# Next round's gather ahead of the up products, and split transfers for a turn's last couple, in a one-core hybrid decoder layer

## The reference, cut to what matters

```python
def per_sequence(args):
    hs, cs = args                                   # hs (256, 1024), cs (256, 32): weight of each expert, 0 if not chosen
    a = jnp.einsum('sd,edf->sef', hs, w_gate)       # w_gate, w_up (32, 1024, 256)
    u = jnp.einsum('sd,edf->sef', hs, w_up)
    act = jax.nn.silu(a) * u * cs[..., None].astype(hs.dtype)
    return jnp.einsum('sef,efd->sd', act, w_down)   # w_down (32, 256, 1024)
```

## Time and profile before

| | |
|---|---|
| device time, median of 3 runs | 353.47 us (353.11 to 355.06) |
| the profiled execution: device time / span | 353.66 us / 351.8 us |
| TensorE busy / VectorE / ScalarE / GpSimd | 90% / 48% / 35% / 13% of the span |
| DMA | 121.07 MB, mean 344 GB/s over the span |
| first gate matmul of the expert loop | 150.54 us |
| first matmul of the last pass / end of its downs | 329.84 us / about 341.85 us |

### The profile page before, as it was taken

One profiled execution on the slowest core, in us unless ns is written; L12 is line 12 of the kernel. 1 busy time (PEld: TensorE's weight loads), 2 busy tenths in 40 slices (PEclk: granted clock), 3 DMA queues, 4 the chain that ended last, 5 costly groups with the idle time before them and its releaser, 6 DMA issues.

```text
span 351.8 us, 11516 instructions
## 1 busy us (share of the span) xinstructions
PE 316.0 (90%) x4758; PEld 246.2 (70%) x4759; DVE 167.3 (48%) x461; ACT 121.4 (35%) x308; POOL 46.8 (13%) x82
## 2 busy tenths in 40 slices
PE   8999999999999999978799899999999849686582
PEld 6999899799774446666577677777777537556250
DVE  4868275554264513754345355555555422251333
ACT  2725264454254227333233133333333211220213
POOL 3300002632504037800000000000000000000001
PEclk9999999999999999999999999999999976898999
DMA  7999995081749998699999999999999999999953
GB/s 271 328 360 386 387 391 215 32 328 38 321 149 388 300 400 334 238 286 392 420 410 396 415 420 408 417 420 414 427 411 422 408 415 422 414 422 416 416 208 119
DMA packets 34709, 121.07 MB, mean 344 GB/s; under 512 B 5640, under 2 KB 10144, under 8 KB 27520
## 3 DMA queue, kind: packets, MB, share of 16 engines
q1 hardware_dynamic: 34352, 120.63, 88.1%
q10 hardware_dynamic: 336, 0.14, 0.1%
HBM read 119.72 MB, written 1.05 MB: 343 GB/s over the span
## 4 chain that ended last, share of the span: by engine, by line
PE 72%; DMA 11%; SPq 10%; issue 3%; ACT 2%; DVE 1%; POOLq 0%; POOL 0%; ACTq 0%; DVEq 0%
PE bank L815 13%; PE bank L555 13%; PE bank L622 7%; DMA spare<-in_w_up_dram 6%; PE bank L847 6%; PE bank L770 6%; DMA ring<-in_w_up_dram 5%; SPq L397 5%; PE bank L549 5%; PE bank L777 3%; SPq L409 2%; SPq L391 2%; PE bank L569 2%; PE bank L531 2%; PE bank L584 1%
## 5 line engine op out<-in xcount | busy, mean ns | idle before, releaser
L815 PE MATMUL bank<-ring,hT 128*32 128x128 f32 x1664 | 56.5, 290 | 15.1 <-DMA ring<-in_w_up_dram 7.5
L815 PEld LDWEIGHTS bank<-ring,hT 128*32 128x32 f32 x1664 | 49.6, 117 | 24.3 <-issue 24.1
L1557 DVE SCALAR_TENSOR_TENSOR yb<-bank,pp,yb 64x512 fp32r<-64x512 f32 x34 | 25.5, 750 | 47.8 <-ACT yb L1085 47.2
L1271 DVE TENSOR_TENSOR unit_lo<-ring,unit_hi 128x2048 fp32r<-128x2048 f32 (+1 forms) x12 | 26.5, 2209 | 24.0 <-ACT unit_hi L917 24.0
L770 PEld LDWEIGHTS bank<-pp,qk 128*128 128x128 bf16 x912 | 29.6, 101 | 7.4 <-issue 5.6
L1085 ACT ACTIVATE yb<-bank,pp 64x512 fp32r<-64x512 f32 x34 | 23.2, 683 | 32.3 <-PE bank L847 31.9
L770 PE MATMUL bank<-pp,qk 128*128 128x64 bf16 x912 | 31.9, 197 | 2.6 <-issue 2.6
L622 PE MATMUL bank<-ring,qk 128*128 128x512 f32 (+1 forms) x72 | 29.9, 551 | 0.0
L1233 POOL TENSOR_SCALAR stats<-qk 128x1 f32<-128x1 f32 x2 | 0.6, 310 | 197.2 <-ACT work L1105 197.2
L1540 DVE SCALAR_TENSOR_TENSOR pp<-bank,stats,pp 128x128 f32<-128x128 f32 x18 | 6.3, 351 | 43.0 <-ACT pp L1074 43.0
L815 PE MATMUL bank<-work,hT 128*32 128x128 f32 x320 | 19.7, 273 | 6.7 <-DMA spare<-in_w_up_dram 4.2
(11 more groups left out here) (217 smaller groups left out, 529.5 us busy)
## 6 DMA issues: line engine op xcount, KB each, us to landing
ring<-in_w_up_dram SPq DMA_DIRECT2D x24, 1024.0 KB, 17.2
ring<-in_w_down_dram SPq DMA_DIRECT2D x24, 1024.0 KB, 17.6
ring<-in_w_gate_dram SPq DMA_DIRECT2D x16, 1024.0 KB, 16.2
ring<-in_w_in_dram SPq DMA_DIRECT2D x4, 2048.0 KB, 17.3
ring<-in_w_gate_dram SPq DMA_DIRECT2D x16, 512.0 KB, 14.4
ring<-in_w_out_dram SPq DMA_DIRECT2D x4, 1024.0 KB, 13.7
spare<-in_w_gate_dram SPq DMA_DIRECT2D x4, 1024.0 KB, 18.7
spare<-in_w_up_dram SPq DMA_DIRECT2D x4, 1024.0 KB, 19.6
```

What stands on the lines that cost most here:

```text
L815: last = mm(p_gu[b:b + CAP, w * P:(w + 1) * P], hg[:, k, CAP * e:CAP * (e + 1)], w_gu[at[e]][:, w, k, h, :], start=(k == 0), stop=(k == KD ...
L1271: V.tensor_tensor(unit_lo[b][:, k, :], unit_src(u)[:, k, :], unit_hi[b][:, k, :].bitcast(fp32), ALU.subtract).then_inc(w_lo_ready, 1)
L1557: V.scalar_tensor_tensor(out=yb[half][rest, :], in0=p_y[rows, :], scalar=wcol[rows, :], in1=yb[half][rows, :].bitcast(fp32), op0=ALU.mult, ...
```

## The change

In TensorE's pass the gather of the next pass, with the read of `base` and the wait for `sel_ready` ahead of it, moves from behind the ups to between the small matmuls (L825) and the ups. Behind the ups come the selections, then `add_result`, and only then the wait for `act_ready` and the transpose. VectorE's and ScalarE's programs are the same. For the last couple of a turn the ups and the downs of each expert are loaded in two transfers of 512 KB instead of one of 1 MB: first the first halves of both experts, then the second ones, each half with a semaphore of its own, and TensorE waits for the second halves in the middle of the ups and of the downs.

```diff
+        dn2_in = {p: sem(f"dn2_in{p}") for p in places(TURN - 1)}
+        up2_in = {p: sem(f"up2_in{p}") for p in places(TURN - 1)}
...
+            def load_up_part(e, p, part):
+                c = slice(part * KD // 2 * FE, (part + 1) * KD // 2 * FE)
+                src = I["w_up"][0, bass.ds(e, 1)].rearrange("o (p k) f -> p (o k f)", p=P)
+                up = gu_at[p].rearrange("p (w c) -> p w c", w=2)[:, 1]
+                sp.dma_start(up[:, c], src[:, c]).then_inc((up_in, up2_in)[part][p], 16)
+
+            def load_dn_part(e, p, f):
+                src = I["w_down"][0, bass.ds(e, 1), f * P:(f + 1) * P].rearrange("o p n -> p (o n)")
+                sp.dma_start(w_dn[p][:, f], src).then_inc((dn_in, dn2_in)[f][p], 16)
...
                     sp.wait_ge(used, passed)
+                    if w == 1 and loads[0][1] in places(TURN - 1):
+                        for part in range(2):
+                            for e, p in loads:
+                                load_up_part(e, p, part)
+                        continue
...
                 sp.wait_ge(down_done, passed)
-                for e, p in loads:
-                    load_dn(e, p)
+                if loads[0][1] in places(TURN - 1):
+                    for f in range(2):
+                        for e, p in loads:
+                            load_dn_part(e, p, f)
+                else:
+                    for e, p in loads:
+                        load_dn(e, p)
...
                         if w == 0 and k == KD // 2:
                             pe.wait_ge(hg_ready, i + 1)
+                        if w == 1 and k == KD // 2 and at == places(TURN - 1):
+                            for e in range(2):
+                                pe.wait_ge(up2_in[at[e]], fillings * 16)
...
                         picked.then_inc(rr_done, 1)
-                pe.wait_ge(base_ready, 1)
-                pe.reg_load(edge, base[0:1, bass.ds(q + 1, 1)])
-                pe.wait_ge(sel_ready, i + 2)
-                gather(p_hg).then_inc(gathered, 1)
+
+                        pe.wait_ge(base_ready, 1)
+                        pe.reg_load(edge, base[0:1, bass.ds(q + 1, 1)])
+                        pe.wait_ge(sel_ready, i + 2)
+                        gather(p_hg).then_inc(gathered, 1)
                 pe.wait_ge(rrow_ready, i + 1)
                 pe.wait_ge(selw_ready, i + 1)
...
+                add_result(i)
                 pe.wait_ge(act_ready, i + 1)
                 nc.tensor.transpose(p_tr[:, 2 * P:3 * P], act_sb, ident).then_inc(actt_done, 1)
-                add_result(i)
                 pe.wait_ge(actT_ready, i + 1)
-                for e in range(2):
-                    pe.wait_ge(dn_in[at[e]], fillings * 16)
                 for f in range(2):
+                    if f == 0 or at == places(TURN - 1):
+                        for e in range(2):
+                            pe.wait_ge((dn_in if f == 0 else dn2_in)[at[e]], fillings * 16)
```

More of the change, by code:

```diff
@@ L405, in load_gu, with load_up @@
                     load_half(e, p, 0)
-                load_half(e, p, 1)
-            def load_dn(e, p):
-                sp.dma_start(w_dn[p], I["w_down"][0, bass.ds(e, 1)].rearrange("o (h p) n -> p (o h) n", p=P)).then_inc(dn_in[p], 16)
+                load_up(e, p)
+            def load_up(e, p):
+                if p in places(TURN - 1):
+                    load_up_part(e, p, 0)
+                    load_up_part(e, p, 1)
+                else:
+                    load_half(e, p, 1)
+            def load_up_part(e, p, part):
[6 more added lines that the diff above has]
+                sp.dma_start(w_dn[p][:, f], src).then_inc((dn_in, dn2_in)[f][p], 16)
+            def load_dn(e, p):
+                if p in places(TURN - 1):
+                    load_dn_part(e, p, 0)
+                    load_dn_part(e, p, 1)
+                else:
+                    sp.dma_start(w_dn[p], I["w_down"][0, bass.ds(e, 1)].rearrange("o (h p) n -> p (o h) n", p=P)).then_inc(dn_in[p], 16)
             def load(e):
@@ L445, in _ @@
             sp.wait_ge(lo_ready, LAST)
-            load_half(RINGED, RINGED, 1)
+            load_up(RINGED, RINGED)
             sp.wait_ge(acc_set, 1)
```

## The result

The changed kernel takes 362.41 us (median of 4 runs, 361.5 to 364.74), the kernel before 354.26 us (median of 4, 353.11 to 357.14). The ratio is 1.0236, with a 95% interval from 1.0179 to 1.0293: the change makes the kernel 2.4% slower, where 3.8% (367 us) was forecast, inside the range of 359.5 to 374. The profiled execution, the slowest of the four, took 364.74 us, with a span of 362.9 us, 11.1 us longer than before.

A forecast was written before the change was run, and what follows sets the result against it. The loop was taken as transfer-bound, TensorE close behind. Last downs end at 150.54 + 11.50 + 17 x 11.23 + 2.0 + 0.2 = 355.2; adding 9.95 and 1.86 gives 367 us, 3.8% slower, range 359.5 to 374.

The forecast's parts named there:

- The bound moves from the transfers to TensorE's wait for the selection: Expert loop: TensorE, chained to VectorE's selection at G + 3.66 (G: gates' start), becomes the bound, idling 1.8 us a pass.
- A pass of 11.23 us: TensorE's pass, gates to next gates: 11.23 us instead of 8.73, bounds 10.95 and 11.4.
- the hand-overs: Delays between engines in a pass: 0.15 us from selection to gather, 0.14 us from ScalarE's copy to the downs.
- No room for 2.5 us a pass: Expert loop: TensorE's present waits for weights cannot absorb the longer passes; last downs start after 200.7 us, not 189.4.
- the rival: Expert loop: not slower, transfers stay the bound if passes stay under about 10.4 us; 352.5 us, chance 0.04.
- Stops of the instruction stream, 2.0 us: Passes 1 to 5: "issue" stops come once, partly hidden in new idle times; 2.0 us taken, bounds 0 and 7.1.
- the first pass's later selection: First pass: its selection ends at G + 3.93 (G: gates' start), so that pass takes 11.50 us.
- The clock as a rival: TensorE in the loop: the clock falls, one pass in three losing 2.7 us; 382 us, chance 0.06.
- a sign of being wrong: TensorE in the loop: a clock under 1.00 would show the forecast wrong.
- The queue runs dry at the double pass: Between second and third couples' refills: engines stand still some 2 us, free in the main forecast; rival about 355 us, chance 0.05.
- The split transfers: Last couple's ups and downs in halves: worth nothing at 11.23 us a pass, as TensorE does not wait for weights.
- The estimate of 24 us: Refills: by the skill page's fixed cost, the twelve more transfers would cost 24 us if none overlapped.

The follow-up runs named there:

- taking the wait away from the changed kernel: The whole change plus VectorE making the next selection ahead of the previous result's second part, against the kernel before: 354.29 us, ratio 0.9985.
- The earlier selection alone: Kernel before, with only VectorE's selection made ahead of the previous result's second part, run twice: ratios 0.9955 and 0.9995.
- the halves with the earlier selection: Kernel before, with the split transfers and VectorE's selection ahead of the previous result's second part: ratio 0.9993.

## Why the prediction was right, point by point

**The bound moves from the transfers to TensorE's wait for the selection: right.** The selection was forecast at 3.66 us after the gates and came at 3.68; the idle time before the gather at 1.8 us and measured 1.67; the gather's start at 3.81 and measured 3.74. That this wait is the loss is shown by four runs: the gather alone has it in full (1.042), the halves alone have none of it (0.996), the sums alone cost little (1.0057, 1.0007 to 1.0108), and taking the wait away from the changed kernel takes the loss away (0.9985). Of the 2.32 us by which a pass is longer, that last run takes back 1.83 us (11.05 to 9.22). The other 0.49 us is what the sums' new place costs alone (8.73 to 9.20); it is paid only while TensorE is the bound.

**A pass of 11.23 us: right in kind, 0.20 us too long.** From the fourth pass's start at 187.26 to the eighteenth's at 341.69 it is 11.03 us on average. The terms that were mis-sized are the hand-overs and the sums: the gather starts 0.06 us after the selection (212.99 to 213.05), not 0.15, the downs start 0.05 us after ScalarE's copy (218.57 to 218.62), not 0.14, and the sums take 1.01 us from start to start, not 1.12. On the other side the gather took 1.50 us instead of 1.41. In 17 passes that is 3.4 us; with the 1.3 us of the point after next on the other side, 367.0 becomes 364.9, and 364.74 was measured in the profiled execution. The other 2.3 us, down to the median of 362.41, are a matter of which execution was profiled: the forecast took it for one near the median, and it was the slowest, with the lowest mean clock (0.986; the others 0.990, 0.994 and 0.994). With the measured pass and neither stops nor a fall of the clock the sum would be 367.0 - 3.4 - 2.0 = 361.6 us, and the two executions at 0.994 took 361.5 and 361.65; they have no profile, so that this is argued and not shown. The row in attention from which the hand-over of 0.14 us was taken stood ahead of another kind of matmul; it was a poor stand-in.

**No room for 2.5 us a pass: right, and the threshold fits.** Passes of 8.73, 9.20 and 9.22 us leave the time within 0.7% of before, passes of 11.05 and 11.44 us do not; 10.4 us was named as the limit. The cases in between were not tried. An estimate from the changed kernel's trace says about the same: its last gates were there 6.7 us early, 0.4 us for each of the 17 passes ahead of them, so that passes of some 10.6 us would have used that up. The 352.5 us that the rival gave for such passes were not reached: with passes of 9.22 us it was 354.29 us, and the last gates landed at 331.77, not 329.7.

**Stops of the instruction stream, 2.0 us: the wrong term, near in size by luck.** The changed kernel's profile has no such stop in its first passes, nor has that of the gather alone; it seems that they fell into the new idle times entirely. Instead, passes 1 and 2 took 12.82 and 12.85 us, 3.6 us more than two quiet passes: 3.1 us because their gathers and ups ran partly at the clock's lower level (gathers of 2.43 and 1.72 us from start to start instead of 1.50, ups of 2.50 and 3.27 us instead of 1.89), and 0.4 us because the selection came later in both. For the first pass's later selection and the stops together 2.3 us were forecast: 1.3 us less. The changed kernel with whole transfers had the other case: clock 1.00 from 152 to 172 us, one stop of 0.73 us, and a span of 361.6 instead of 362.9 us.

**The clock as a rival: it had the wrong place.** It was priced for every third pass of the loop, and a clock under 1.00 in the loop was named as a sign of being wrong. That sign came: the clock was at 0.83 from 152 to 172 us, and the forecast of the time has no term for it. It fell in the first two passes alone, behind waits for the selection of 1.89 and 1.88 us. These waits are not enough by themselves, since the changed kernel with whole transfers had two of 1.88 us there and kept 1.00. From 186 us on it stayed at 1.00 in every stretch shown, in spite of 1.67 and 0.35 us of idle time in each pass. In the late passes the clock is better than before (1.00 against 0.86), since the long waits for weights are gone.

**The queue runs dry at the double pass, at no cost: right.** From 186 to 192 us the DMA share is 0.51 at 173 GB/s. It ran low earlier too (a share of 0.60 from 159 to 162 us), in the first refill: not foreseen, and as free. The ups' transfers now wait for the first gather and the ups behind it, and went out at 159.57 us instead of 156.13; but with whole transfers and the clock at 1.00 they went out at 158.64 us and the share stayed at 1.03, so that it took the fall of the clock as well. One sign did not come: the DMA share was to be under 0.5 before the last pass, and it was 1.02 from 335 to 341 us; it fell only 2.3 us into the last pass, at about 344 us.

**The split transfers: right.** They are worth nothing in the changed kernel (362.41 us with them, 363.31 us without). The 0.9 us in the order of before were expected ahead of that run and are not part of this prediction. The estimate of 24 us from the Trainium skill's page "DMA: Bandwidth & Descriptors" (a fixed 2 us for each transfer, if none overlapped; the page's section on the anatomy gives it for transfers issued from GpSimd) does not hold in the full queue of SyncE here: 416 GB/s with the halves.

## What to carry to other kernels

Before an instruction is moved ahead, look up when its input is finished, counted from a point that the move doesn't shift: here the selection came 0.22 us before its use, so that there was no room for even a small step forward, and the producer's order on its own engine had to change first. Work put into a wait that exists at the end of a run is paid for in every pass where that wait does not exist. Where two resources are near each other, work out the pass time at which the bound changes sides; under it an uncovered 0.5 us a pass costs little (0.6% here, 0.1 to 1.1%), above it every tenth is multiplied by the number of passes.

## What the runs showed of the hardware that was not expected

The same kernel can have one of two first turns. The earlier selection alone was profiled twice, with spans of 351.2 and 355.6 us. Busy time by stretch, of the first and of the second:

```profile
172.00:182.00 10.00, 10.00 (x217) 6.95 (x213) 4.81 (x16) 3.10 (x9) 0.00 (x0) 1.00 1.01 413
182.00:194.00 12.00, 12.00 (x305) 9.26 (x301) 6.24 (x18) 4.55 (x12) 0.00 (x0) 1.00 0.95 376
```
```profile
172.00:182.00 10.00, 10.00 (x199) 6.26 (x198) 3.16 (x9) 2.48 (x6) 0.00 (x0) 0.75 1.01 415
182.00:194.00 12.00, 12.00 (x235) 8.37 (x235) 6.63 (x23) 3.51 (x11) 0.00 (x0) 1.00 0.71 278
```

In the second, behind a stop of the instruction stream of 2.56 us in pass 2, the clock went to its lower level of 1.2 GHz for some 6 us. The third couple's gates are then released later, just where the queue is nearly empty, and the DMA engines are idle for 0.29 of 12 us instead of 0.05, 2.9 us more, which a kernel bound by its transfers never gets back. In the first the stop was 2.28 us and the clock stayed. The length of the stop does not decide it: the split transfers alone had one of 2.56 us too and kept the clock, and the halves with the earlier selection had one of 2.28 us and lost it (0.77). Another 1.4 us of the difference of 4.4 us lie at the end, behind the wait for the last ups: these 64 matmuls took 3.34 us in the second and 1.95 us in the first.

Of the twelve profiles of this case, seven have the clock under 1.00 somewhere from 152 to 182 us. Leave out the four kernels that gather ahead of the ups in every pass: of the other eight profiles, the four that kept the clock have spans of 350.9 to 351.8 us, and the four that lost it 353.0 to 355.6 us. That this is also what spreads the kernel before over 353 to 357 us is likely, and only argued: its slower runs have no profile. Their mean clocks lean the same way; of the 29 executions beside the second group of runs, the ten with a mean clock of 0.976 or more have a median of 354.3 us, the ten at 0.970 or less one of 356.4 us. It also bounds what these comparisons can tell to about 0.4%. The changed kernel is not hurt by a dry queue, only by the slower passes themselves.
